# Final additions laced with low parts, two up slabs taken chunk by chunk, and spread gate sums moved, in a 19-stage float32 transformer kernel

## What is computed

```python
x = x + 0.5 * swiglu_ffn(rms_norm(x, g[0]), ffn_w_in[i, 0], ffn_w_out[i, 0])   # eight of this form, 2816 hidden columns
...
h = h + mixers[i % N_MIXERS](rms_norm_3(h, attn_norms[i]), *mixer_args[i])     # i = 1: fox_mixer
h = h + peer_ffn(rms_norm_3(h, ffn_norms[i]), *peer_args[i])
...
def fox_mixer(x, w_in, f_bias, w_out):
    ...
    log_f = jax.nn.log_sigmoid(proj[..., 3 * ATTN_WIDTH:].astype(jnp.float32) + f_bias.astype(jnp.float32))
    c = jnp.cumsum(log_f, axis=1).transpose(0, 2, 1)
    ...
        s = jnp.einsum('bhqd,bhkd->bhqk', qb, k).astype(jnp.float32) + cb[..., None] - c[:, :, None, :]
        p = masked_softmax(s, pos[None, :] <= t[:, None])
        return jnp.einsum('bhqk,bhkd->bhqd', p.astype(v.dtype), v)
```

## Time and profile before

| | |
|---|---|
| median of three executions | 4585.19 us (lowest 4583.04, highest 10304.64) |
| the profiled execution | 4591.12 us |
| its span, first to last instruction | 4589.8 us |
| mean granted TensorE clock | 0.953 of full |
| PE busy | 4317.9 us, 94% of the span |
| DVE busy | 3068.8 us, 67% |
| ACT busy | 1961.7 us, 43% |
| POOL busy | 112.8 us, 2% |
| bytes read from HBM | 671.48 MB, 147 GB/s over the span |

### The profile page before, as it was taken

The page is one execution under the profiler, slowest core; times in us unless marked ns, Lnnn a source line. Parts: engine busy times, 40 slices in busy tenths (PEclk is TensorE's granted clock), DMA queues, the critical chain, the costliest instruction groups (busy, mean ns, idle before and its releaser), DMA issues.

```text
span 4589.8 us, 71848 instructions
## 1 busy us (share of the span) xinstructions
PE 4317.9 (94%) x30760; PEld 3979.4 (87%) x30760; DVE 3068.8 (67%) x4411; ACT 1961.7 (43%) x2499; POOL 112.8 (2%) x112
## 2 busy tenths in 40 slices
PE   8989999899998999979888899999999899999998
PEld 7778888787886888858786899999998799999998
DVE  6567675676766766457435699846855589954964
ACT  5345453454535544455324443243244444234233
POOL 0000000000003000020000000000000000000000
PEclk9989999899998999979975999999999999999999
DMA  5424544244541545415331354354353245245343
GB/s 215 175 97 156 184 174 174 90 178 161 184 156 56 185 174 189 159 46 186 141 120 38 129 183 149 115 186 160 111 185 138 105 171 184 103 165 184 111 159 145
DMA packets 94701, 679.29 MB, mean 148 GB/s; under 512 B 11296, under 2 KB 11952, under 8 KB 12848
## 3 DMA queue, kind: packets, MB, share of 16 engines
q1 hardware_dynamic: 91152, 662.74, 39.7%
q0 software_dynamic: 1024, 7.61, 0.4%
q10 hardware_dynamic: 2208, 4.34, 0.3%
HBM read 671.48 MB, written 3.17 MB: 147 GB/s over the span
## 4 chain that ended last, share of the span: by engine, by line
PE 82%; DVE 12%; ACT 3%; POOL 1%; issue 1%; DMA 0%; ACTq 0%; DVEq 0%; POOLq 0%; SPq 0%
PE psum L621 21%; PE psum L550 14%; PE psum L551 14%; PE psum L552 14%; PE psum L622 10%; PE psum L1155 3%; DVE slab_low L1590 2%; DVE room L2211 1%; DVE room L2227 1%; DVE x L1707 1%; DVE room L2209 1%; DVE room L2213 1%; PE psum L792 1%; PE psum L572 1%; POOL room L2259 1%
## 5 line engine op out<-in xcount | busy, mean ns | idle before, releaser
L1590 DVE TENSOR_TENSOR slab_low<-slab,slab_high 128x2048 fp32r<-128x2048 f32 x632 | 1449.2, 2293 | 802.0 <-ACT slab_high L1174 798.8
L1174 ACT ACTIVATE slab_high<-slab 128x2048 fp32r<-128x2048 f32 x632 | 1203.9, 1905 | 539.3 <-PE psum L622 259.1
L550 PE MATMUL psum<-h_parts,slab_high 128*128 128x256 f32 x3424 | 997.1, 291 | 66.8 <-DVE h_parts L1633 61.6
L621 PE MATMUL psum<-h_parts,slab_high 128*128 128x512 f32 x2816 | 1004.8, 401 | 40.4 <-DVE h_parts L1668 40.4
L551 PE MATMUL psum<-h_parts,slab_high 128*128 128x256 f32 x3424 | 982.6, 287 | 0.0
L552 PE MATMUL psum<-h_parts,slab_low 128*128 128x256 f32 x3424 | 981.8, 287 | 0.0
L622 PE MATMUL psum<-h_parts,slab_low 128*128 128x256 f32 x2816 | 793.6, 282 | 0.0
L550 PEld LDWEIGHTS psum<-h_parts,slab_high 128*128 128x128 f32 x3424 | 671.1, 196 | 79.8 <-issue 67.7
L621 PEld LDWEIGHTS psum<-h_parts,slab_high 128*128 128x128 f32 x2816 | 533.8, 190 | 174.8 <-issue 19.8
L551 PEld LDWEIGHTS psum<-h_parts,slab_high 128*128 128x128 f32 x3424 | 671.4, 196 | 2.0 <-issue 1.9
L552 PEld LDWEIGHTS psum<-h_parts,slab_low 128*128 128x128 f32 x3424 | 670.9, 196 | 0.0
(11 more groups left out here) (292 smaller groups left out, 4772.6 us busy)
## 6 DMA issues: line engine op xcount, KB each, us to landing
slab<-in_up SPq DMA_DIRECT2D x176, 1024.0 KB, 4.8
slab<-in_keys_up SPq DMA_DIRECT2D x128, 1024.0 KB, 4.8
slab<-in_keys_down SPq DMA_DIRECT2D x128, 1024.0 KB, 4.8
slab<-in_down SPq DMA_DIRECT2D x88, 1024.0 KB, 4.8
slab<-in_w_in SPq DMA_DIRECT2D x16, 1024.0 KB, 4.8
slab<-in_wq SPq DMA_DIRECT2D x16, 1024.0 KB, 4.8
slab<-in_w_pw SPq DMA_DIRECT2D x12, 1024.0 KB, 4.8
slab<-in_w_qkv SPq DMA_DIRECT2D x12, 1024.0 KB, 4.8
```

Of the source, the lines that this page charges most:

```text
L550: nc.tensor.matmul(out, lhs[0], rhs[0], start=first, stop=False, **options)
L621: nc.tensor.matmul(out, lhs[0], rhs, start=first, stop=False, **options)
L1174: nc.scalar.activation(k.high[m % PARTS][:, 0:width], k.slabs[m % RING][:, 0:width], ACT.Copy).then_inc(k.rounded.up())
L1590: nc.vector.tensor_tensor(k.low[m % RING][:, 0:width], k.slabs[m % RING][:, 0:width], k.high[m % PARTS][:, 0:width], ALU.subtract).then_in ...
```

## The change

Three edits, and what they need.

1. **Final additions laced.** DVE no longer makes the final additions of ffn, peer and fox at the stage's end. It keeps them as a function `finish(j)` and makes them in the next stage: where that is an ffn or fox, pair j stands just ahead of the low parts of chunks 2j and 2j+1 (`early_input`); elsewhere all four stand at the stage's entry (`finish_x`), which leaves the order as it was. This moves instructions at three borders: ffn to ffn (stages 4 and 11) and peer to fox (17). In `add_down`, the operation is a TENSOR_TENSOR in place of a SCALAR_TENSOR_TENSOR with scale 1.
2. **Slabs 0 and 1 chunk by chunk.** In an ffn, PE takes slab 0 and slab 1 together: chunk c of slab 0 (both halves), then chunk c-2 of slab 1. In fox, slab 0 is taken chunk by chunk for both halves in tick 0, and tick 1 has no product. The `ones` sums thus stand behind slab 1 in an ffn.
3. **fox's small pieces.** DVE's L2011 moves ahead of the slab's low part in its tick; scores no longer wait for v; items 8 to 15 start at other ticks.

```diff
-    v.starts = [8, 9, 10, 11, 12, 13, 14, 15, 18, 19, 20, 21, 24, 24, 25, 25]
+    v.starts = [8, 9, 10, 11, 12, 13, 14, 15, 16, 17, 18, 19, 22, 23, 24, 25]
...
         for f in range(FC):
-            high, low = self.take()
-            w = [part.rearrange("p (a k n) -> p a k n", a=2, k=DC) for part in (high, low)]
+            if f >= 2:
+                w = [part.rearrange("p (a k n) -> p a k n", a=2, k=DC) for part in self.take()]
...
-                self.x_read(3 if k.first_pair and at == 0 else at)
+                self.x_read(3 if k.first_pair and at == 0 or f >= 2 else at)
...
-            for a in range(2):
-                for c in range(DC):
-                    if f == 0 and a == 0:
-                        nc.tensor.wait_ge(k.h_ready.sem, k.h_ready.at(c + 1))
-                    mm = self.product_wide(pair[:, a], [part[:, a, c, :] for part in w], k.h[:, c], c == 0, c == DC - 1)
-            mm.then_inc(k.slab_done.up())
+            if f == 0:
+
+                firsts = [[part.rearrange("p (a k n) -> p a k n", a=2, k=DC) for part in self.take()] for _ in range(2)]
+                pairs = [k.bank_pairs[g + k.first_pair].rearrange("p e (a t) -> p e a t", a=2) for g in range(2)]
+                for step in range(DC + 2):
+                    if step < DC:
+                        nc.tensor.wait_ge(k.h_ready.sem, k.h_ready.at(step + 1))
+                    for g in range(2):
+                        c = step - 2 * g
+                        if not 0 <= c < DC:
+                            continue
+                        for a in range(2):
+                            mm = self.product_wide(pairs[g][:, a], [part[:, a, c, :] for part in firsts[g]], k.h[:, c], c == 0, c == DC - 1)
+                        if c == DC - 1:
+                            mm.then_inc(k.slab_done.up())
...
             if f == 0:
                 nc.tensor.wait_ge(k.squares_added.sem, k.squares_added.at(3))
...
-            nc.tensor.wait_ge(k.evacuated.sem, k.evacuated.at(2 * group + 2))
+            nc.tensor.wait_ge(k.evacuated.sem, k.evacuated.at(2 * group + 1))
             nc.tensor.wait_ge(k.columns_scaled.sem, k.columns_scaled.at(group + 1))
+
+        def values(it):
+            nc.tensor.wait_ge(k.evacuated.sem, k.evacuated.at(2 * (it["pair"] // 2) + 2))
...
-        for j in range(DC // 2):
+        pair_done, all_done = [k.pair_done.at(j + 1) for j in range(3)], k.slab_done.at(FC + FC // 2)
+
+        def finish(j):
             both = k.x[:, 2 * j:2 * j + 2, :]
             if j < 3:
-                nc.vector.wait_ge(k.pair_done.sem, k.pair_done.at(j + 1))
+                nc.vector.wait_ge(k.pair_done.sem, pair_done[j])
...
-            add.then_inc(k.x_done.up())
+            add.then_inc(k.x_done.sem)
+        self.finish = finish
+        k.x_done.later(DC // 2)
...
     def early_input(self, gain):
-        k, nc = self.k, self.k.nc
+
+        k, nc = self.k, self.k.nc
+        ready, value = k.x_ready(0)
+        if ready is not k.x_done:
+            nc.vector.wait_ge(ready.sem, value)
         for c in range(DC):
+            if c % 2 == 0:
+                self.finish(c // 2)
             nc.vector.wait_ge(k.h_rounded.sem, k.h_rounded.at(c + 1))
...
             self.shift(v, tick)
+            if 7 <= tick < 7 + NP:
...
+                nc.vector.wait_ge(k.decay_made.sem, k.decay_made.at(pair + 1))
...
+                add.then_inc(k.decayed.up())
+                nc.vector.wait_ge(k.decayed.sem, k.decayed.at(pair + 1))
             if half == 0 and n < len(v.jobs) + DC // 2:
                 self.rest_slab()
```

More of the change, by code:

```diff
@@ L862, in project_half @@
         w = [part[:, 0:DC * width].rearrange("p (k n) -> p k n", k=DC) for part in self.pair]
+        if n == 0:
+            for c in range(DC) if half == 0 else ():
+                nc.tensor.wait_ge(k.h_ready.sem, k.h_ready.at(c + 1))
+                for a in range(2):
+                    mm = self.product(bank[:, a * T:(a + 1) * T], [part[:, c, a * P:(a + 1) * P] for part in w], (k.h[:, c, 0, :], k.h[:, c, 1, :]),
+                                      c == 0 and a == 0, c == DC - 1, skip_group_check=True)
+            if half == 0:
+                mm.then_inc(k.slab_done.up())
+            return
         cols = slice(half * P, (half + 1) * P)
         for c in range(DC):
-            if n == 0 and half == 0:
-                nc.tensor.wait_ge(k.h_ready.sem, k.h_ready.at(c + 1))
             h = k.h[:, c, 0, :], k.h[:, c, 1, :]
@@ L902, in sums, with attend @@
         mm.then_inc(k.summed.up())
-    def attend(self, v, tick, inputs):
+    def attend(self, v, tick, inputs, values):
         k, nc = self.k, self.k.nc
@@ L981, in fox @@
                 mm.then_inc(k.decay_made.up())
-            self.attend(v, tick, inputs)
+            self.attend(v, tick, inputs, values)
     def nsa(self, v):
@@ L1985, in fox @@
             self.shift(v, tick)
+            if 7 <= tick < 7 + NP:
+                pair = tick - 7
+                made = k.banks[3].rearrange("p (b t) -> p b t", b=2)
+                causal = k.const("causal").unsqueeze(1)
+                nc.vector.wait_ge(k.decay_made.sem, k.decay_made.at(pair + 1))
+                for i in range(TT):
+                    keys = P * (i + 1)
+                    add = nc.vector.scalar_tensor_tensor(out=v.decay[:, 2 * pair:2 * pair + 2, P * i:P * i + keys], in0=made[:, :, 0:keys], scalar=0.125,
+                                                         in1=causal[:, :, P - i * P:T].to_broadcast([P, 2, keys]), op0=ALU.mult, op1=ALU.add)
+                add.then_inc(k.decayed.up())
+                nc.vector.wait_ge(k.decayed.sem, k.decayed.at(pair + 1))
             if half == 0 and n < len(v.jobs) + DC // 2:
@@ L2405, in program @@
             pool.fox(v)
+    dve.finish_x()
     sp.store()
```

53 lines of the change are left out of this document (28 added, 25 removed).

## The result

The changed kernel took 4566.62 us in the median (4559.27 to 4567.88), beside 4588.65 for the kernel before in the same session: ratio 0.9943, 95% interval 0.9928 to 0.9958. That is no change by the 2% bound, and 26 us (19 to 33) less. The two medians lie only 22 us apart, since that of before still counts one execution of 10304.64 us, which the ratio leaves out. The forecast was 4568 us, a gain of 17.3. In a second session the changed kernel, as it stands, came to 0.9967 (0.9956 to 0.9979), a gain of 15 us (10 to 20). The forecast gain lies between the two. The two profiled executions differ by 31.8 us (spans 4589.8 and 4558.0). That is more than either ratio says, and the experiments show where part of it comes from.

The account below looks back on a forecast made before the run. PE was taken as the bound, busy 94% of the span, so gains come only from its holes and lower clock. Terms summed to 17.3 us, giving a forecast median of 4568 us, with 8 in 10 between 4553 and 4586.

Parts of the forecast that it names:

- stage 8: The ffn behind a norm: 21.0 us laced against 20.8 before, forecast gain -0.2 us.
- stage 1: The very first ffn: bias lines wait until 40.6 behind the sums, plus 2.0 for the clock; forecast -7.7 us.
- stages 4, 11: The two ffn behind an ffn: PE begins 3.1 us sooner, sums wait 2.8 us; forecast gain about 2.0 us together.
- fox, spread sums: Fox's reads of spread gate sums moved ahead end 5.2 us of waits and restore the clock; forecast gain 10.5 us.
- Mixer-fed ffn: Stages 3, 6, 10, 13: waits at the sums go, slab 3 waits 1.9 us; forecast gain 13.1 us together.
- the chain of 7.5 us: In an ffn, from first sum matmul to the end of slab 3's low part; slab 2 alone covers 5.65 us.
- The rival for slower: Clock falls behind every new hole in seven stages, 10 to 21 us, time 4578 to 4589; chance 0.15.
- the forecast case: The whole kernel gains as the summed terms say, with times from 4560 to 4577 us; chance 0.5.
- The long form of POOL's additions: Stages 4 and 11: first square to last addition taken as 7.4 us, rather than a chain of 5.5.
- Fox, entry: Laced additions delay fox's sums; PE idles 5.5 us instead of 1.4, plus 1.0 for the clock: forecast -4.9 us.
- Fox, items: Items started one per tick lose 5.4 us of mutual waits; scores wait for keys at two ticks: forecast gain 4.5 us.

Follow-up runs that it names:

- edit 3 alone: Only fox's changes (reads ahead of the slab's low part, values' own wait, one item started per tick) on the kernel before: ratio 0.9960.
- reads behind: The changed kernel with fox's reads of the spread gate sums back behind the slab's low part: ratio 0.9995.
- edit 2 alone: Only ffn slabs 0 and 1 chunk by chunk together, and fox's slab 0 chunk by chunk, on the kernel before: ratio 0.9979.
- squares between: The changed kernel with ACT's squares of a pair directly behind its high parts in stages 4, 11 and fox: ratio 0.9935.
- The experiment: The changed kernel with the bias table's memset ahead of DVE's input and its load ahead of ACT's root: ratio 0.9950, stage 1 217.7 us.
- Edit 1 alone: Only the final additions laced with the next input's low parts, PE's order as before, on the kernel before: ratio 1.0026.

## Why the prediction was right, and where it was not

Each term against the stage lengths. Before is the mean of three profiles (before twice, edit 3 alone), changed that of three (changed twice, reads behind); fox is split at the first and last spread sums, with edit 2 alone in place of edit 3 for the two later parts of before, and the changed kernel's two profiles for those of changed.

| term | before | changed | gain | forecast |
|---|---|---|---|---|
| stages 3, 6, 10, 13 | 195.3, 204.3, 194.4, 217.4 | 189.3, 200.5, 189.3, 213.3 | 12.6 (19.0 less two borders of 3.2) | 13.1 |
| stage 8 | 202.2 | 201.5 | 0.7 | -0.2 |
| stage 1 | 219.7 | 227.6 | -7.9 | -7.7 |
| stages 4, 11 | 203.8, 202.7 | 204.3, 205.8 | 2.8 (with the borders) | 2.0 |
| fox, to the first spread sums | 32.6 | 38.4 | -5.0 (with the border's 0.7) | -4.9 |
| fox, spread sums | 46.6 | 34.4 | 12.2 | 10.5 |
| fox, rest | 95.2 | 88.4 | 6.8 | 4.5 |

They add up to 22.2 us against a forecast of 17.3, and to 0.9952, between the two measured ratios. The means still carry steps of 2 to 3 us in pace and clock of each execution, so a term is known to 1 or 2 us at best.

Up to slab 3, where the forecast was made, these steps hardly count. There stages 3, 6, 10 and 13 gain 13.7 together, stage 8 0.1 and stage 1 -8.3, as in the table within 1.1. Stages 4 and 11 gain only 0.5 together, not 2.8: all three profiles of the changed order ran stage 4 at the quicker pace, and none of the three of before did. With 0.5 the sum is 20.0 us and the ratio 0.9956. That the total came so near the forecast is in part luck: 1.5 us too much for stages 4 and 11 stand against 1.7 too little for the spread sums.

**Mixer-fed ffn.** Right in mechanism and size: no wait for POOL, the chain of 7.5 us uncovered by one slab. What was missing is where it is paid: at the mean, ahead of slab 2, not ahead of slab 3. The price is the same since both stand on one chain. No clock fell behind these holes of 0.6 us, in four profiles of four stages each. In stage 13 the low stretch behind the old hole, there in all profiles with that hole, is gone in all without it. The rival for slower came true only in part: behind the sums' wait of 2.6 us in stages 4 and 11 the clock did fall, for 3.4 us in three profiles of four, and it cost 0.6 to 1.0 us a stage, where the rival needed 2.5 in seven stages. The Trainium skill ("TensorE: Matmul & The Clock Gate", section "HAM oscillation — how this bites in real kernels") warned of it; the holes of 0.6 us here did not bring it, those of 1.6 to 2.2 us that recur in fox did.

**Stage 1.** The hole was read right (40.6, it came at 40.86; 40.6 is 5.6 behind 35.00, which the prediction put as 5.7). The clock behind it was sized at 2.0: in the first profile slab 2's first 9 products took 0.29 us longer each, 2.6 us, and the two bias matmuls 1.2, so nearer 4 and some 10 in all up to there. The mean over profiles holds less, 7.9, and up to slab 3 8.3. In the other three profiles of the changed order the clock fell 1.2 to 1.5 us sooner in the hole, so more of the 10.2 us at half clock lay where PE had no work. The experiment shows that all of it hangs on one memset and one load.

**Stages 4 and 11.** PE started 3.2 us sooner (3.1 said) and the sums waited 2.6 to 2.7 (2.8 said). In the first profile, where the clock stayed full, slab 3 had a hole of 0.8, and the two stages gained 1.9 together up to slab 3, as forecast (2.0). In the others the clock fell behind the sums' wait, a cost that the forecast case put at nothing here, and next to no gain is left. Edit 1 alone shows what the forecast didn't say: the laced additions are worth having at these borders only with edit 2, and lose some 4 us a stage without it. The long form of POOL's additions, 4.68 for two, was the right choice; with squares between, each took 1.3.

POOL's second L2309 fell beside DVE's slab subtraction, both inputs in SBUF, and the two took 4.68 us; beside DVE's additions, one input in PSUM, each took 1.30. The Trainium skill ("SBUF — State Buffer", section "Who interferes with whom") draws the line just there: a DVE instruction with two SBUF inputs contends with POOL's reads, one with at most one (outside DVE's two-port modes, which the page treats apart) doesn't. The trace agrees with both halves.

**Fox, entry.** 5.0 against 4.9. Of my two parts the wait is right (5.5 us, as said). The clock fell within it, for 10.2 us in all, 7.6 of them behind the wait (by the two product times of stage 1 an estimated 3.4 us lost), which costs more than the 1.0 that I allowed; but the second profile of before and that of edit 3 alone had half clock there too, 6.8 us at the sums, where the first profile had none, so the cost over their mean is smaller. In this changed kernel edit 1 therefore loses more in fox, 5.0, than it gains in stages 4 and 11, until the squares are moved.

**Fox, spread sums.** The mechanism, that the clock comes back with the waits, is shown by the reads put back: of their 12.4 us, 11.6 are in that part (46.0 us instead of 34.4). The term was 1.7 too small; 0.6 of that I had allowed for new waits, and none came.

**Fox, items.** The items' waits in ticks 24 to 31 fell from 5.4 to 0.6 us, and the part behind the spread sums came out 5.3 us shorter than in the first profile of before (93.7 to 88.4). With the reads put back and the new starts kept it took 89.8, 3.9 less. The 6.8 in the table holds a low stretch of one profile, so 4.5 was about right. No run has the new starts alone.

**What stays open.** Why an execution runs a stretch of matmuls at another pace at the same granted clock, and where in a stage half clock falls when no wait has changed, is not explained. The two sessions' ratios, 0.9943 and 0.9967, differ by more than their intervals lead one to expect, and this scatter is the likely cause, but that was not shown.

## What to carry to other kernels

A few microseconds of wait that recur in a row cost twice when the array's clock falls with them: in fox 5.5 us of waits were worth 12. Before lacing work on one engine with another's, count what the consumer has to do for each piece that arrives, since edit 1 alone lost 4 us in each of stages 4 and 11, and with edit 2's second slab between lost nothing there. And count what hangs on the pieces that come last: in fox the later squares cost 5 us. When one slab less covers a chain, look at everything that hangs on its far end; a memset and a small load that nobody had to place late cost 8 us. And compare stage by stage over more than one profile: unchanged stages moved by up to 14 us together.

## What the runs showed of the hardware

- At a granted clock of 1.00 and with no idle time, PE started 427 matmuls of 128x256 in 50 us in three executions (two of before, one of the changed kernel) and 444 in another of the changed kernel. In an ffn, the matmul behind a 512-wide one started 231 or 235.5 ns after it, by stage and execution, in before and changed alike.
- POOL's addition of two 128x512 tiles took 1.30 us beside a DVE addition from PSUM, and two took 4.68 us where the second fell beside DVE's subtraction of a 128x2048 slab, which kept its 2.29 us.
- In the hole of 6.7 us in stage 1 the granted clock fell to half before PE resumed and stood there for 10.2 us each time (four profiles of the changed order). In fox's hole of 5.5 us it fell too, for 10.2 us in three profiles and 6.8 in one. With 2.6 us of wait at the sums of stage 4, the clock stayed full in one profile and fell for 3.4 us in three. Behind holes of 0.6 us in stages 3, 6, 10 and 13 it never fell.
